# A decoder layer on one core: gate and up of the feed-forward from seven products of quadrants, with the second norm in the same block

## The reference

```python
D_MODEL = 1024
D_FF = -(-8 * D_MODEL // (3 * 256)) * 256      # 2816
...
    x = x + merged @ w_out[l]
    h2 = rms_norm(x, norm2_g[l])
    x = x + (jax.nn.silu(h2 @ w_ffn_gate[l]) * (h2 @ w_ffn_up[l])) @ w_ffn_down[l]
```

## Time and profile before

| | |
|---|---|
| median of three runs | 2356.65 us (2356.05 to 2357.43) |
| the profiled execution | 2357.6 us, its span 2355.8 us, so 1.8 us lie around the span |
| PE busy | 2198.6 us, 93% of the span, 10352 matmuls |
| DVE, ACT, POOL busy | 1196.6, 601.1, 780.2 us (51%, 26%, 33%) |
| mean granted TensorE clock | 0.975 of full speed |
| norm 2 block and feed-forward | from about 1596 us to the end |

### The profile page before, as it was taken

How to read it: one execution, slowest core, us unless ns; L and a number is a source line. 1 busy time by engine, 2 the same in 40 slices (tenths; PEclk the granted TensorE clock), 3 DMA queues, 4 the chain that set the end, 5 groups by cost and what they waited for, 6 DMA issues and landing times. The chain is left out here.

```text
span 2355.8 us, 29150 instructions
## 1 busy us (share of the span) xinstructions
PE 2198.6 (93%) x10352; PEld 1769.1 (75%) x10352; DVE 1196.6 (51%) x1644; ACT 601.1 (26%) x1046; POOL 780.2 (33%) x630
## 2 busy tenths in 40 slices
PE   4999989898799999999999799997999999999998
PEld 3787768687677777777777588875888888888887
DVE  4557585851366567567556655555233233322224
ACT  3224241420245445445445300012100000000000
POOL 3222131312243434434435233323333333233331
PEclk9999999999999999999999899997999999999999
DMA  3211111212322431431442722212111111111111
GB/s 103 51 27 47 34 45 27 54 45 81 81 65 52 98 66 50 98 76 40 98 76 63 296 75 75 85 36 72 45 54 45 53 45 37 43 53 53 53 45 71
DMA packets 159681, 153.87 MB, mean 65 GB/s; under 512 B 8064, under 2 KB 135040, under 8 KB 159632
## 3 DMA queue, kind: packets, MB, share of 16 engines
q1 hardware_dynamic: 157904, 150.07, 23.5%
q10 hardware_dynamic: 1728, 3.15, 0.3%
HBM read 107.06 MB, written 20.97 MB: 54 GB/s over the span
## 5 line engine op out<-in xcount | busy, mean ns | idle before, releaser
L123 POOL TENSOR_TENSOR w_hi<-w_raw,w_ones 128x64 fp32r<-128x64 f32 x88 | 35.0, 397 | 767.4 <-PE gla_g L147 366.9
L473 POOL TENSOR_TENSOR sb_rows<-sb_beta,sb_rest 128x128 f32<-128x128 f32 (+7 forms) x128 | 167.0, 1309 | 253.1 <-DVE sb_rest L824 253.1
L126 POOL TENSOR_TENSOR w_lo<-w_raw,w_hi 128x1024 fp32r<-128x1024 f32 x88 | 218.8, 2486 | 7.3
L824 DVE TENSOR_TENSOR_SCAN sb_rest<-sb_rest 128x128 f32<-128x128 f32 (+7 forms) x128 | 202.5, 1590 | 36.4 <-ACT sb_beta L675 36.4
L830 DVE TENSOR_TENSOR sb_wt_lo<-sb_t,sb_wt_hi 128x512 fp32r<-128x512 f32 x192 | 106.3, 554 | 173.3 <-ACT sb_wt_hi L683 171.4
L123 POOL TENSOR_TENSOR ffw_hi<-ffw_raw,ffw_ones 128x64 fp32r<-128x64 f32 x66 | 23.9, 363 | 471.7 <-PE ff_down L1724 250.9
L1776 DVE TENSOR_TENSOR y<-ff_down,y 128x512 f32<-128x512 f32 x176 | 121.7, 691 | 111.5 <-PE ff_down L1724 111.1
L1761 DVE TENSOR_TENSOR ff_act<-ff_up,ff_act 128x512 f32<-128x512 f32 x44 | 30.4, 692 | 269.6 <-PE ff_up L147 269.6
L126 POOL TENSOR_TENSOR ffw_lo<-ffw_raw,ffw_hi 128x1024 fp32r<-128x1024 f32 x66 | 165.2, 2503 | 5.5
L147 PE MATMUL sb_g<-h_hi,w_hi 128*128 128x512 f32 x544 | 161.4, 421 | 3.7 <-DVEq L728 3.7
L147 PE MATMUL sb_g<-h_lo,w_hi 128*128 128x512 f32 x544 | 157.5, 414 | 0.0
(11 more groups left out here) (208 smaller groups left out, 4573.6 us busy)
## 6 DMA issues: line engine op xcount, KB each, us to landing
w_raw<-w_in SPq DMA_DIRECT2D x64, 512.0 KB, 8.4
ffw_raw<-w_ffn_gate SPq DMA_DIRECT2D x22, 512.0 KB, 3.8
ffw_raw<-w_ffn_up SPq DMA_DIRECT2D x22, 512.0 KB, 3.9
ffw_raw<-w_ffn_down SPq DMA_DIRECT2D x22, 512.0 KB, 3.3
sb_qs<-sb_q_st SPq DMA_DIRECT2D x32, 256.0 KB, 5.1
sb_kh<-sb_k_st SPq DMA_DIRECT2D x32, 256.0 KB, 5.0
sb_kl<-sb_k_st SPq DMA_DIRECT2D x32, 256.0 KB, 5.0
mp_sig<-gates_t SPq DMA_DIRECT2D x16, 512.0 KB, 4.3
```

The source lines that it names most:

```text
L123: self.nc.gpsimd.tensor_tensor(hi[:, 0:64], raw[:, 0:64], self.ones[:], ALU.mult)
L126: self.nc.gpsimd.tensor_tensor(lo, raw, hi, ALU.subtract).then_inc(self.ready, 1)
L473: nc.gpsimd.tensor_tensor(rows[tb // 4][:, tb % 4, 0:width], beta[:, n % 2, 0:width], rest[:, n % 2, 1:width + 1], ALU.mult).then_inc(row_ ...
L824: nc.vector.tensor_tensor_scan(back, back, back, 1.0, ALU.mult, ALU.bypass).then_inc(scanned, 1)
```

## The change

`feed_forward` and the second `norm_transposed` are replaced by one block, `norm_and_feed_forward`. Gate and up are computed with the seven products of Winograd's form of Strassen's scheme: for a chunk of 256 hidden columns the weights W (1024 x 256) are cut into four quadrants of 512 x 128 (contraction half by f-tile), the transposed activations into four of 512 x 512 (contraction half by token half). Where the plain way takes eight products of quadrants for gate and eight for up, this takes seven each, 14 products of 3 passes x 4 = 12 matmuls. Four of the seven take sums of activation quadrants (t1 to t4), made once in the norm; four take sums of weight quadrants, made in every chunk.

**POOL** makes the weight sums (four instructions for gate, four for up, 128x512, in place in the raw tiles) and the low parts of the 14 weight operands and of four pieces of w_down; in the norm it makes the low parts of t1 to t4. **ACT** makes all high parts of weights (which POOL made before), copies six product banks to SBUF (`keep`), and does the sigmoids and roundings. **DVE** makes t1 to t4 and the other low parts in the norm, adds product banks to the copies, multiplies, and adds the down banks to y as before. The ring of split weights has six slots of 128x512, and ACT fills the slot of product i+6 when product i has ended. Raw weights have a buffer of 1 MB each for gate, up and down: SP loads gate's next when product 12's low part is made, up's when 13's is, down's when its fourth low part is.

**PE** does P1, P2, P3, P5, P6, P7, P4, each for gate and then for up (numbered 0 to 13 here), then the down product of the same chunk, 96 matmuls as before but with token tiles 4 to 7 ahead of 0 to 3. The first down group waits for `y_low` 3 (the low parts of three of the four hidden quadrants), the fifth for the fourth. The banks of P3 and P2 are also the down banks. P6, P7 and P4 add onto P1's bank. In the first chunk POOL's order is: low parts of t for column pairs 0 and 1, four weight sums, low parts for pair 2, low parts of P1 and P2, those of pair 3, the other four sums, then P3 and so on. t1 to t4 have one buffer (`t_tmp`), so DVE's sum for the next pair waits for POOL's low part of the one before.

SP stores y in sixteen transfers of 256 KB. The SBUF set aside for POOL-made DMA descriptors is cut to 2048 bytes; no DMA is started by POOL before or after.

```diff
+def norm_and_feed_forward(nc, c, ssq, y, gain, w_gate, w_up, w_down, out):
...
+    NP = 14
...
+    P1, P2, P3, P5, P6, P7, P4 = range(7)
...
+            t_tmp = sb("t_tmp", [P, 4, KH, P], stack=norm)
...
+        w_hi = [sb(f"w_hi{i}", [P, KH, P], F32R) for i in range(RING)]
...
+        X, Y, A, E = [[ps(f"{n}_{m}") for m in "gu"] for n in ("x", "y", "a", "e")]
+        down = [E[0], E[1], A[0], A[1]]
...
+        ROW = {P1: (0, 0), P2: (0, 1), P3: (0, 1), P5: (1, 0), P6: (0, 0), P4: (1, 1)}
...
+                def low(slot, m, p, count):
+                    pool.wait_ge(w_high, count)
+                    nc.gpsimd.tensor_tensor(w_lo[slot][:], operand(m, p), w_hi[slot][:], ALU.subtract
+                                            ).then_inc(w_ready, 1)
+                def sums_1(m, ch):
+                    (a11, a21, a22) = (raw[m][:, 0:KH, 0:P], raw[m][:, 0:KH, P:PAIR], raw[m][:, KH:KT, P:PAIR])
+                    pool.wait_ge(raw_loaded[m], 16 * ch + 16)
+                    nc.gpsimd.tensor_tensor(s_tmp[m][:], a11, a21, ALU.subtract).then_inc(s_made, 1)
+                    pool.wait_ge(s_made, 8 * ch + 2 * m + 1)
+                    nc.gpsimd.tensor_tensor(a21, a21, a22, ALU.add).then_inc(s_made, 1)
...
+                def gate_up(ch, slot, at, norm=lambda pair: None):
+                    norm(0)
+                    norm(1)
+                    for m in (G, U):
+                        sums_1(m, ch)
+                    norm(2)
+                    for n, p in enumerate((P1, P2, P3, P5, P6, P7, P4)):
+                        for m in (G, U):
+                            low(slot(2 * n + m), m, p, at + 2 * n + m + 1)
+                        if p == P2:
+                            norm(3)
+                            for m in (G, U):
+                                sum_2(m, ch, at)
+                            for m in (G, U):
+                                sum_4(m, ch, at)
...
+                with pool.Fori(0, N - 1, 1) as ch:
+                    down_low(ch)
+                    gate_up(ch + 1, lambda n: ring(4 + n), first(ch) + SLOTS_PER)
+                down_low(N - 1)
...
+                def gate_up(ch, slot):
+                    for i in range(NP):
+                        act.wait_ge(gu_done, NP * ch + i + 1)
+                        if i < 2:
+                            keep((cg[0], u[0])[i], X[i])
+                        if i == 4:
+                            sigmoid(0, ch)
+                        if i == 5:
+                            y_round(0, ch)
+                        if i in (6, 7):
+                            keep((cg[0], u[1])[i - 6], Y[i - 6])
+                        if i == 8:
+                            keep(cg[1], X[G])
+                        if i == 9:
+                            act.wait_ge(y_low, 4 * ch + 1)
+                            keep(u[0], X[U])
+                        if i == 10:
+                            sigmoid(1, ch)
+                            y_round(1, ch)
+                        if i == 11:
+                            sigmoid(2, ch)
+                        if i < 8:
+                            high(slot(i + 6), i + 6, ch)
+                        elif i < 12:
+                            down_high(i - 8, ch)
+                        if i == 12:
+                            y_round(2, ch)
+                            sigmoid(3, ch)
+                        if i == 13:
+                            y_round(3, ch)
...
+                for pair in range(PP):
+                    if pair == 2:
+                        for n in range(4):
+                            high(n, n, 0)
+                    norm_high(pair)
+                for n in range(4, RING):
+                    high(n, n, 0)
+                gate_up(0, lambda n: n % RING)
+                with act.Fori(0, N - 1, 1) as ch:
+                    for n in range(2):
+                        act.wait_ge(gu_done, NP * ch + NP - 1 + n)
+                        high(ring(4 + n), n, ch + 1)
+                    for n in range(2, 6):
+                        act.wait_ge(d_done, ND * ch + 8 * (n // 2))
+                        high(ring(4 + n), n, ch + 1)
+                    gate_up(ch + 1, lambda n: ring(4 + n))
...
+                    for n, (o, a, b) in enumerate(((t1, copied, b11), (t3, b22, copied), (t2, b22, t1), (t4, b21, t2))):
+                        if n < 2:
+                            dve.wait_ge(b12_kept, pair + 1)
+                        if n != 2:
+                            dve.wait_ge(b_high, 3 * pair + (1, 2, 0, 3)[n])
+                        need(dve, t_low, 4 * (pair - 1) + n + 1)
+                        if n >= 2:
+                            dve.wait_ge(t_made, 4 * pair + (1, 3)[n - 2])
+                        tt(o, a, b, ALU.subtract).then_inc(t_made, 1)
...
+                def gate_up(ch):
+                    product_done(2, ch, 1)
+                    tt(cg[0][:], A[G][:], cg[0][:], ALU.add).then_inc(c_step, 1)
+                    product_done(3, ch, 2)
+                    tt(u[0][:], A[U][:], u[0][:], ALU.add).then_inc(c_step, 1)
+                    step(ch, 2, u[0], u[0], cg[0], ALU.mult)
+                    hidden(0, ch)
+                    y_low_part(0, ch)
+                    product_done(8, ch, 5)
+                    tt(cg[1][:], Y[G][:], cg[1][:], ALU.add).then_inc(c_step, 1)
+                    step(ch, 4, cg[1], E[G], cg[1], ALU.add)
+                    product_done(9, ch, 6)
+                    tt(u[0][:], Y[U][:], u[0][:], ALU.add).then_inc(c_step, 1)
+                    step(ch, 6, u[0], E[U], u[0], ALU.add)
+                    step(ch, 7, u[0], u[0], cg[1], ALU.mult)
+                    product_done(10, ch, 0)
+                    tt(cg[0][:], X[G][:], cg[0][:], ALU.add).then_inc(c_step, 1)
+                    hidden(1, ch)
+                    y_low_part(1, ch)
+                    product_done(11, ch, 0)
+                    tt(u[1][:], X[U][:], u[1][:], ALU.add).then_inc(c_step, 1)
+                    step(ch, 10, u[1], u[1], cg[0], ALU.mult)
+                    hidden(2, ch)
+                    y_low_part(2, ch)
+                    dve.wait_ge(sig_ready, 4 * ch + 4)
+                    tt(cg[1][:], X[G][:], cg[1][:], ALU.mult).then_inc(c_step, 1)
...
+                for s in range(4):
+                    scale(s)
+                for pair in range(PP):
+                    if pair == PP - 1:
+                        low(pair, 0)
+                        combine(pair)
+                        low(pair, 1)
+                        low(pair, 2)
+                    else:
+                        combine(pair)
+                        for n in range(3):
+                            low(pair, n)
+                    if pair < 2:
+                        scale(2 * pair + 4)
+                        scale(2 * pair + 5)
...
+                def multiply(slot, bank, op):
+                    start = op in (P1, P2, P3, P5)
+                    passes = ((w_hi, 0), (w_hi, 1), (w_lo, 0))
+                    for n, (w, part) in enumerate(passes):
+                        for k in range(KH):
+                            ins = nc.tensor.matmul(bank[:], w[slot][:, k, :], h[op][part][:, k, :],
+                                                   start=(start and n == 0 and k == 0), stop=(n == 2 and k == KH - 1),
+                                                   skip_group_check=not start)
+                    ins.then_inc(gu_done, 1)
+                def gate_up(ch, slot, at, norm=False):
+                    for n, p in enumerate((P1, P2, P3, P5, P6, P7, P4)):
+                        if norm:
+                            if n < 3:
+                                pe.wait_ge(b_low, 3 * (PP - 1) + n + 1)
+                            else:
+                                pe.wait_ge(t_low, 4 * (PP - 1) + (1, 3, 3, 4)[n - 3])
+                        for m in (G, U):
+                            pe.wait_ge(w_ready, at + 2 * n + m + 1)
+                            bank = {P1: X, P2: A, P3: E, P5: Y, P6: X, P7: X, P4: X}[p][m]
+                            if p == P2:
+                                need(pe, d_free, 4 + ND * ch - 1 + m if not norm else 0)
+                            if p == P3:
+                                need(pe, d_free, 4 + ND * ch - 3 + m if not norm else 0)
+                            if p == P6:
+                                pe.wait_ge(kept, 6 * ch + 1 + m)
+                            if p == P7:
+                                pe.wait_ge(kept, 6 * ch + 5 + m)
+                            if p == P4:
+                                pe.wait_ge(c_step, STEPS * ch + 9 + m)
+                            multiply(slot(2 * n + m), bank, p)
+                def down_block(ch):
+                    for n, (nh, t) in enumerate(D_GROUPS):
+                        if n % 8 == 0:
+                            pe.wait_ge(w_ready, d_first(ch) + 2 * nh + 2)
+                        if n == 0:
```

(53 more changed lines are left out.)

338 lines of the change are left out of this document (228 added, 110 removed).

## The result

The changed kernel takes 2293.88 us in the median of four runs (2291.68 to 2294.87), the kernel before 2356.72 beside it (2356.05 to 2357.43): a ratio of 0.9732, 95% interval 0.9715 to 0.9749. That is faster by 62.8 us where 56.1 were forecast, and 0.12 us under the low end of the range. The profiled execution took 2291.68 us.

The account below looks back on a forecast made before the run. PE, busy for 93% of 2355.8 us, was taken as the bound. Terms -59.8 -6.8 +1.0 +9.2 +0.3 = -56.1 us took the profiled execution from 2357.6 to 2301.5, forecast median 2301 us, range 2294 to 2316.

Parts of the forecast that it names:

- Matmuls taken away: Gate and up in 11 chunks: 264 fewer matmuls at 0.2267 us, -59.8 us; a steady chunk from 65.28 to 59.84.
- The end: Last down product: no wait of 3.94 us and no low clock costing 2.90 us, -6.8 us.
- The norm: Second norm to PE's first product: POOL's low parts and sums come late, PE starts at 1633.5, not 1624.27: +9.2 us.
- P3 in the first chunk: First chunk: PE wants P3 13.7 us after its start, POOL needs 14.0: +0.3 us.
- The wait ahead of down: Each chunk's first down group: last needed low part about level with PE's request, 0.1 us a chunk, +1.0 us.
- The walk of DVE and POOL: Chunk's end, from product 10: POOL holds DVE's two-SBUF-input instructions; quadrant 2's low part is done at 7.8 us.
- The first rival: Down product waits in every chunk, 0.5 to 1.2 us each: 2306 to 2314 us, say 2308; chance 0.32.
- The step that failed: Start of the norm: DVE's first scaling stays at 1600.71, when the gain lands; no change in time ahead of it.
- faster POOL waits: Norm: POOL's waits for DVE fall short of the walk, PE starts near 1628.3: 2295 us; chance 0.08.
- dear POOL: Norm, first chunk and steady chunks: POOL's strided instructions cost about 1.6 us each: 2325 us; chance 0.10.
- larger gain: Norm: POOL waits less for DVE than walked, PE starts near 1628.3: 2295 us; chance 0.08.

Follow-up runs that it names:

- e13: Changed kernel, with POOL's low part of the fourth w_down piece waiting for DVE's low part of hidden quadrant 2: 2292.5 us.
- e7: Changed kernel, with POOL's first four weight sums moved: gate's two ahead of the first norm pair, up's two ahead of the second: 2287.80 us.
- e1: Kernel before, with only the 32-byte tile ssq allocated ahead of the shared weights: 2345.83 us against 2355.62.
- e3: Changed kernel, padded so that the shared weights start 32 bytes past a multiple of 64 again: 2302.42 us.
- e8: Changed kernel, with ACT's fourth rounding of down weights placed ahead of the third sigmoid behind product 11: 2296.72 us.
- e9: Kernel of e8, with POOL also waiting for y_low 4 before the next chunk's first four weight sums: 2295.03 us.
- e6: Changed kernel, with 32 bytes ahead of activations h, so that h, the weight ring, y_hi and y_lo all start 32 past a multiple of 64: 2292.02 us.
- e4: Changed kernel, with 32 bytes of padding ahead of the new block's weight ring, moving y_hi and y_lo too, h staying: 2303.94 us.
- e5: Changed kernel, with only activations h moved to 32 past a multiple of 64, the weight ring staying: 2300.75 us.

## Why the prediction missed, step by step

- **Matmuls taken away: right.** 59.84 us a chunk forecast, 60.03 in the trace with the wait, 59.85 in e13 without it, at a granted clock of 1.00. The isolated gap of the Trainium skill (TensorE: Matmul & The Clock Gate, Back-to-back issue gap), by which the saving would have been 57.0, lost to the row again: 0.2267 us.
- **The end: right.** 0.12 us in place of 3.94 ahead of the last down product, and no low clock behind it. The term that was left out, the last store of 256 KB, shows as 3.17 us from PE's end to the end of the span in place of 3.75.
- **The norm: right, a little small.** +9.2 forecast; first scaling to first product 33.55 us and not 23.56, so +10.0. POOL's 128x512 costs 1.28 and not 1.20 us, 1.4 us over 17 instructions; the wait between pairs was forecast at 2.4 and is 2.41. e7 shows that POOL is the late one, by taking 3.4 us off it.
- **P3 in the first chunk: undersized.** +0.3 forecast; PE waits 1.23 us, since POOL's eight low parts and four sums cost more, and the product behind the wait takes 2.98 and not 2.72: +1.5.
- **The wait ahead of down: right in kind and place, half in size.** 0.1 us a chunk forecast and 0.19 there, 1.9 us in ten chunks. The walk of DVE and POOL held: the low part of quadrant 2 is held by POOL, as e13 proves. What was too small is PE's side: the weight load was taken to start some 0.2 us ahead of its matmul, and un-held it starts 0.39 ahead (e13), so PE asks earlier than walked. The first rival's 0.5 to 1.2 us didn't come.
- **The step that failed:** "DVE's first scaling still starts at 1600.71, when the gain lands". It starts at 1588.34. The sum took the time of everything ahead of the changed block as given, because the diff changes no instruction there. But the diff moves one 32-byte tile ahead of the shared weights, and that ends a mismatch of 32 bytes between the two operands of matmuls in untouched blocks. e1 has that move alone, 9.8 us; e3 takes it out of the changed kernel again, 8.5 us. The two profiled executions show more, 12.4 us, since they are no medians: the one of before is 0.9 us over its median and the one of after 2.2 under, which leaves 9.3. Of the new block itself the sum was nearly right: from the gain's load to the end of the span before takes 759.4 us and after 705.8, 53.6 less where the sum had 56.1.

The rivals of faster POOL waits (2295) and of dear POOL (2325) didn't happen: the norm costs more than forecast, not less, and POOL's low parts take 1.28 us and not 1.20, its un-held sums 1.27 to 1.31 and not 1.10, far from 1.6. That the total of 2293.88 comes near the "larger gain" case (2295) is chance: it has another cause. Without the layout the range would have held, as e3's 2302.42 does.

The terms add up in the traces: -12.4 (start) -59.8 -6.8 +10.0 +1.5 +1.9 -0.6 (end of the span) = -66.2 us, and the spans differ by 2355.8 - 2289.7 = 66.1. The medians differ by 62.8, as the profiled execution was the fastest of its four.

## What to carry to other kernels

A diff acts on code that it doesn't touch through where it puts the tiles: write down where each shared matmul operand starts, before and after, and give both operands of a matmul the same remainder by 64 bytes (0 and 32 are what was tried here, at 128x512 in fp32r). Where two engines shut each other out, moving work away can put another instruction into the gap (e8) or move the hold to one ahead (e9), so hold back the one that does the harm, and judge by when the waited-for instruction ends. Where an edit's gain is smaller than the scatter of what runs ahead of it, read the stage's own distance in the trace (60.03 to 59.85) and not the median.

## What the runs showed of the hardware

- A 128x128 by 128x512 matmul follows the one before after 0.2267 us when both operands begin, by the order of allocation, in the same half of 64 bytes (both at 0: changed kernel, e1; both at 32: e6), and after 0.2333 when in different ones (merge before, e3, e4, e5), at a granted clock of 1.00. Why is open.
- POOL's 128x512 subtraction or addition takes 1.27 to 1.31 us un-held, with its pieces apart in the raw tile as with contiguous ones (L1750 from the raw tile 1288 ns, from the contiguous sum 1292 and 1287).
- A DVE instruction with two SBUF inputs behind a POOL instruction is held to its end and ends some 0.57 us later (POOL's until 1963.67, DVE's until 1964.24).
